# State-space tables of a four-layer trunk: angles doubled inclusively, powers alike, and the early table work reordered

## The reference, cut to what matters

```
step    = exp(log_step)[:, None]                  # 64 groups of 16 channels
lam_bar = exp((a_re + i a_im) * step)             # 64 groups x 64 states, complex
b_bar   = ((lam_bar - 1) / lam)[..., None] * b
bu      = einsum('gpc,sbgc->sbgp', b_bar, u)
states  = associative_scan(x_t = lam_bar * x_{t-1} + bu_t)      # over 256 tokens
y       = real(einsum('gcp,sbgp->sbgc', c, states)) + d_skip * h
z       = gelu(y) @ w_glu + b_glu;  out = z1 * sigmoid(z2)
```

## Time and profile before

| | us |
|---|---|
| median of 3 runs | 1458.84 (1455.54 to 1459.17) |
| the profiled execution's own time | 1456.15 |
| its span | 1454.4 |
| PE busy | 1388.9 (95%) |
| DVE busy | 1015.8 (70%) |
| ACT busy | 801.8 (55%) |
| POOL busy | 654.3 (45%) |

### The profile page before, as it was taken

The page is one execution under the profiler, slowest core; times in us unless marked ns, Lnnn a source line. Parts: engine busy times, 40 slices in busy tenths (PEclk is TensorE's granted clock), DMA queues, the critical chain, the costliest instruction groups (busy, mean ns, idle before and its releaser), DMA issues.

```text
span 1454.4 us, 33002 instructions
## 1 busy us (share of the span) xinstructions
PE 1388.9 (95%) x13677; PEld 1308.2 (90%) x13677; DVE 1015.8 (70%) x1613; ACT 801.8 (55%) x1336; POOL 654.3 (45%) x391
## 2 busy tenths in 40 slices
PE   8999999999998988999998679999999999999998
PEld 8999999989787777999987669999989998999988
DVE  6774987735595465897778776887755675788841
ACT  5586665635551334665653445665655468575642
POOL 4343365541006102495568753365554232355553
PEclk9999999999999999999999799999999999999999
DMA  6533465553433001485554005465555553455553
GB/s 202 187 126 107 155 204 173 182 195 116 144 128 106 5 4 60 145 234 174 182 173 137 2 3 164 156 203 174 178 192 160 160 159 100 152 185 173 187 172 106
DMA packets 208168, 209.59 MB, mean 144 GB/s; under 512 B 7954, under 2 KB 207170, under 8 KB 208034
## 3 DMA queue, kind: packets, MB, share of 16 engines
q1 hardware_dynamic: 207168, 206.21, 43.9%
q0 software_dynamic: 800, 1.46, 0.5%
q10 hardware_dynamic: 66, 0.02, 0.0%
HBM read 206.62 MB, written 1.05 MB: 143 GB/s over the span
## 4 chain that ended last, share of the span: by engine, by line
PE 81%; DVE 9%; ACT 4%; POOL 3%; issue 2%; DMA 0%; ACTq 0%; DVEq 0%; POOLq 0%
PE psum L422 17%; PE psum L424 17%; PE psum L423 17%; PE psum L818 7%; PE psum L599 5%; PE psum L820 4%; DVE x_low L551 2%; POOL work L2422 1%; ACT w_high L397 1%; PE psum L1751 1%; PE psum L1765 1%; DVE work L536 1%; DVE w_low L405 1%; PE psum L1083 1%; PE psum L2568 1%
## 5 line engine op out<-in xcount | busy, mean ns | idle before, releaser
L405 POOL TENSOR_TENSOR w_low<-ring,w_high 128x1024 fp32r<-128x1024 f32 (+1 forms) x185 | 459.1, 2483 | 662.3 <-ACT w_high L397 662.1
L397 ACT ACTIVATE w_high<-ring 128x1024 fp32r<-128x1024 f32 (+1 forms) x368 | 376.4, 1037 | 216.7 <-PE psum L424 124.5
L422 PE MATMUL psum<-x_high,w_high 128*128 128x256 f32 x1728 | 491.0, 284 | 3.6 <-DVE w_low L405 1.4
L424 PE MATMUL psum<-x_high,w_low 128*128 128x256 f32 x1728 | 488.9, 283 | 0.0
L423 PE MATMUL psum<-x_low,w_high 128*128 128x256 f32 x1728 | 488.9, 283 | 0.0
L405 DVE TENSOR_TENSOR w_low<-ring,w_high 128x1024 fp32r<-128x1024 f32 x183 | 296.2, 1620 | 172.9 <-ACT w_high L397 171.7
L422 PEld LDWEIGHTS psum<-x_high,w_high 128*128 128x128 f32 x1728 | 331.6, 192 | 6.0 <-issue 3.1
L423 PEld LDWEIGHTS psum<-x_low,w_high 128*128 128x128 f32 x1728 | 331.7, 192 | 0.0
L424 PEld LDWEIGHTS psum<-x_high,w_low 128*128 128x128 f32 x1728 | 331.6, 192 | 0.0
L818 PE MATMUL psum<-inner,w_high 128*128 128x512 f32 x528 | 187.0, 399 | 0.9 <-DVE w_low L405 0.9
L931 DVE SCALAR_TENSOR_TENSOR work<-psum,par,work 128x255 f32<-128x255 f32 (+1 forms) x352 | 144.6, 472 | 45.9 <-ACT work L850 45.7
(11 more groups left out here) (351 smaller groups left out, 2223.5 us busy)
## 6 DMA issues: line engine op xcount, KB each, us to landing
ring<-in_ffn_w_up_dram SPq DMA_DIRECT2D x88, 1024.0 KB, 5.1
ring<-in_ffn_w_down_dram SPq DMA_DIRECT2D x32, 1024.0 KB, 5.0
ring<-in_dsa_w_in_dram SPq DMA_DIRECT2D x28, 1024.0 KB, 5.2
ring<-in_ffn_w_down_dram SPq DMA_DIRECT2D x16, 768.0 KB, 4.3
ring<-in_rwkv_w_rkv_dram SPq DMA_DIRECT2D x12, 1024.0 KB, 5.0
ring<-in_dsa_w_out_dram SPq DMA_DIRECT2D x8, 1024.0 KB, 5.0
ring<-in_s_w_glu_dram SPq DMA_DIRECT2D x8, 1024.0 KB, 5.3
ring<-in_rwkv_w_out_dram SPq DMA_DIRECT2D x4, 1024.0 KB, 4.9
```

The source lines that it names most:

```text
L397: act.activation(high, raw, ACT.Copy).then_inc(sem("w_rounded", b), 1)
L405: eng.tensor_tensor(low, raw, high.bitcast(F32), ALU.subtract).then_inc(sem("w_split", b), 1)
L422: pe.matmul(out_, lhs[0], rhs[0], start=start, stop=False, skip_group_check=True)
L424: return pe.matmul(out_, lhs[1], rhs[0], start=False, stop=stop, skip_group_check=True)
```

## The change

The grid and the powers are both held as one table with real and imaginary part side by side, and doubled "inclusively": the last entry that is already there is the factor for the next ones, so that no squared factor is kept. A doubling is two multiplications over both parts at once and two sums. The grid's doublings go into parts 5 to 9 (1 and 2 in part 5, 4 in part 6, 8 in part 7; the last one's products in part 8 and its sums in part 9), and its temporary moves to slot 9, so ACT's copies into that slot now wait for `fill_added` 1. `products(1)` moves out of part 10 to a place behind the MLP and ahead of the norm's reciprocal; `coefs(1)` moves behind the norm's scaling. The scan's first turn waits for `fill_added` 1 instead of 3. The four idle transposes go from this norm and stay in layer 1's.

```diff
@@ norm_mean
                 if c == 1:
-                    idle_turns(pe, 4, 3)
+                    idle_turns(pe, 4 if trailing else 0, 3)
@@
-        grid_tmp = work[:, 14, 1536:2048]
+        grid_tmp = work[:, 9, 0:1024]
-        LAST_PART = 11
+        LAST_PART = 10
@@ first_angle
-            for x, value in zip(grid, (1.0, 0.0)):
-                pool_step.mark(pool.memset(x[:, :, 0:1], value))
             pool.wait_ge(sem("angles_ready"), 3)
-            for x, u in ((L8_RE, U_RE), (L8_IM, U_IM)):
-                pool_step.mark(pool.tensor_copy(small(x), small(u + S5_L - 1)))
+            for v, value in ((0, 1.0), (1, 0.0)):
+                pool_step.mark(pool.memset(grid[:, v, :, 0:1], value))
+                pool_step.mark(pool.tensor_copy(grid[:, v, :, 1:2], small((U_RE, U_IM)[v] + S5_L - 1).unsqueeze(2)))
...
+        def angle_products(pool, have):
+            n = min(have, S5_N - 1 - have)
+            shape = [P, 2, S5_H, n]
+            x, dst = grid[:, :, :, 1:1 + n], grid[:, :, :, have + 1:have + 1 + n]
+            t = grid_tmp[:, 0:2 * S5_H * n].rearrange("p (v g n) -> p v g n", v=2, n=n)
+            for out_, v in ((dst, 0), (t, 1)):
+                factor = grid[:, v, :, have:have + 1].unsqueeze(1).to_broadcast(shape)
+                pool_step.mark(pool.tensor_tensor(out_, x, factor, ALU.mult))
             pool.wait_ge(pool_step.sem, pool_step.n)
...
+        def angle_sums(pool, have):
...
+            for v, op in ((0, ALU.subtract), (1, ALU.add)):
+                pool_step.mark(pool.tensor_tensor(dst[:, v], dst[:, v], t[:, 1 - v], op))
+            pool.wait_ge(pool_step.sem, pool_step.n)
@@ s5_angles
-            if part == 6:
+            if part == 5:
                 first_angle(pool)
-                for half in range(2):
-                    double(pool, 1, half)
-            for p, have in ((7, 2), (8, 4), (9, 8)):
+            for p, have in ((5, 1), (5, 2), (6, 4), (7, 8)):
                 if part == p:
-                    square_angle(pool)
-                    for half in range(2):
-                        double(pool, have, half)
+                    angle_products(pool, have)
+                    angle_sums(pool, have)
+            if part == 8:
+                angle_products(pool, S5_N // 2)
             if part == 9:
-                square_angle(pool)
+                angle_sums(pool, S5_N // 2)
@@ s5_pool
-                if f == 1:
-                    for half in range(2):
-                        double(pool, S5_N // 2, half)
@@ s5_act
                 copy_turned_table(i)
+            act.wait_ge(sem("fill_added"), 1)
@@ s5_math: complex_product (six operations) becomes
+            def next_powers(have, last):
...
+                for out_, v in ((dst, 0), (t, 1)):
+                    factor = both[:, v, have - 1:have].unsqueeze(1).to_broadcast([P, 2, have, S5_H])
+                    step.mark(dve.tensor_tensor(out_, x, factor, ALU.mult))
+                dve.wait_ge(step.sem, step.n)
+                tt(dst[:, 0], dst[:, 0], t[:, 1], ALU.subtract)
+                ins = dve.tensor_tensor(dst[:, 1], dst[:, 1], t[:, 0], ALU.add)
@@ s5_tables
-            if part == 10:
-                products(dve, 1)
-                coefs(dve, 1)
@@ turned_in
-                    dve.wait_ge(sem("fill_added"), 3)
+                    dve.wait_ge(sem("fill_added"), 1)
@@ s5_dve
+            coefs(dve, 1)
             products(dve, 2)
@@ the vector engine's program
                 if L % 3 == 2:
+                    products(dve, 1)
                     norm_scale(dve, norm_index(L, 0), "norm_mix", L, in_psum=IN_PSUM)
```

More of the change, by code:

```diff
@@ L2293, in trunk @@
         V_all = work[:, 9, :].rearrange("p (q r z) -> p q r z", q=4, r=2)
-        grid = [work[:, 13, i * 1024:(i + 1) * 1024].rearrange("p (g n) -> p g n", n=S5_N) for i in (0, 1)]
+        grid = work[:, 13, :].rearrange("p (v g n) -> p v g n", v=2, n=S5_N)
         cos_n, sin_n = (work[:, 13, i * 1024:(i + 1) * 1024].rearrange("p (q z) -> p q z", q=4) for i in (0, 1))
         coef = work[:, 14, 0:1536].rearrange("p (v k g) -> p v k g", v=6, k=S5_L)
-        grid_tmp = work[:, 14, 1536:2048]
+        grid_tmp = work[:, 9, 0:1024]
         with_cos = work[:, 8, 0:512].rearrange("p (r z) -> p r z", r=2)
@@ L2313, in trunk @@
         A_RE, A_IM, STEP, SIGMA, TH, TURNS, ANGLE, CO_ARG, DEN, B_RE, B_IM, TMP = range(12)
-        U_RE, U_IM, GROW, MAG_N, MAG_P, L8_RE, L8_IM, ANGLE_A, ANGLE_B = 12, 20, 28, 36, 44, 52, 53, 54, 55
+        U_RE, U_IM, GROW, MAG_N, MAG_P = 12, 20, 28, 36, 44
         FB_RE, FB_DIFF, FB_SUM, GC_RE, GC_DIFF, GC_SUM = range(6)
         S5_DMAS = (6, 4, 4)
-        LAST_PART = 11
+        LAST_PART = 10
         FT_BANKS = (4, 5)
@@ L2373, in first_angle @@
             pool.wait_ge(pool_step.sem, pool_step.n)
[L2375 to L2382, removed]
-            pool.wait_ge(pool_step.sem, pool_step.n)
-            pool.wait_ge(pool_step.sem,
-                         pool_step.mark(pool.tensor_tensor(dst, dst, t, (ALU.subtract, ALU.add)[half])))
@@ L2396, in s5_angles @@
+        def angle_sums(pool, have):
+            n = min(have, S5_N - 1 - have)
+            dst = grid[:, :, :, have + 1:have + 1 + n]
+            t = grid_tmp[:, 0:2 * S5_H * n].rearrange("p (v g n) -> p v g n", v=2, n=n)
+            for v, op in ((0, ALU.subtract), (1, ALU.add)):
+                pool_step.mark(pool.tensor_tensor(dst[:, v], dst[:, v], t[:, 1 - v], op))
+            pool.wait_ge(pool_step.sem, pool_step.n)
         def s5_angles(pool, part):
@@ L2681, in ts @@
                 then(dve.tensor_scalar(out_, x, a, b, op0, op1))
[L2683 to L2690, removed]
+            def next_powers(have, last):
+                both = work[:, 6, U_RE * S5_H:(U_IM + S5_L) * S5_H].rearrange("p (v k g) -> p v k g", v=2, k=S5_L)
+                x, dst = both[:, :, 0:have], both[:, :, have:2 * have]
+                t = table(GROW, 2 * have).rearrange("p (v k) g -> p v k g", v=2)
+                for out_, v in ((dst, 0), (t, 1)):
[4 more added lines that the diff above has]
+                ins = dve.tensor_tensor(dst[:, 1], dst[:, 1], t[:, 0], ALU.add)
                 if last:
@@ L2695, in complex_product @@
                     then(ins)
-            return then, tt, ts, complex_product
+            return then, tt, ts, next_powers
         def s5_tables(dve, part):
-            then, tt, ts, complex_product = s5_math(dve)
+            then, tt, ts, next_powers = s5_math(dve)
             if part == 0:
@@ L2727, in s5_tables @@
                 if part == p:
-                    last = [table(x + have - 1, 1).to_broadcast([P, have, S5_H]) for x in (U_RE, U_IM)]
-                    complex_product(table(U_RE + have, have), table(U_IM + have, have),
-                                    (table(U_RE, have), table(U_IM, have)), last, table(GROW, have), have == 4)
+                    next_powers(have, have == 4)
             if part == 5:
```

## The result

| | median, us | runs | ratio to before (95% interval) |
|---|---|---|---|
| before | 1458.06 | 20 | |
| changed | 1462.5 | 20 | 1.0025 (1.0016 to 1.0034) |

The forecast was 1451 (1446 to 1456), 6.5 us faster. It came out 3.6 us slower by the ratio (0.0025 x 1458; its interval is 2.3 to 5.0 us), and the medians lie 4.4 us apart. This is at the 4.4 us that I had called a measurement's limit, but twenty runs on each side leave no doubt that it is slower.

The account below looks back on a forecast made before the run. PE bounds the whole span, but POOL's table chain bounds the S5 layer's start. States(0) 8.9 us earlier, less 1.0 for the clock and 1.4 for the port, gives 6.5 us off the 1457.4 mean: 1451 (1446 to 1456).

Parts of the forecast that it names:

- POOL's chain: S5 layer's start: less table work before fill 0 and between fills 0 and 1, 12.1 us off the way to fill 1.
- `products(1)` ahead of the reciprocal: In the norm: moved `products(1)` ends at 795.4, the reciprocal waits 1.5 us for it, scaling ends 4.8 us earlier.
- The second, the port: Second cost, beside POOL's parts 5 to 8: DVE's tables end 0 to 4 us later; 1.4 us taken.
- The adding of squares starts at 789.2 and ends at 790.9: DVE ahead of the norm: with `products(1)` gone from part 10, the squares are added from 789.2 to 790.9.
- PE's split waits: PE's waits for weight splits: the 0.4 us for POOL's goes; of DVE's, 0 to 0.9 us comes back, 0 taken.
- The powers: DVE's tables: six dependent operations become two products and two sums, three times; gain 0 to 0.9 us, 0 taken.
- The tie at 754.3: DVE, with its powers some 2 us shorter, is ready at about 754.3, at the same time as POOL's split.
- The clock: PE in the S5 start: turns of hT at half clock cost 2.8 us, states(0) may regain 1.5; cost taken 1.0.
- port lock: Rival: DVE ends its tables 4 us later, PE starves for splits, norm starts 4 us later; 1452.5 to 1455.3, chance 0.15.
- the four signs of being wrong: 960-column POOL products well above 2 us; more than three split waits; reciprocal after 798; half clock in turns of hT.

Follow-up runs that it names:

- g_squares: The changed kernel with one more wait: POOL's additions of fill 0 wait until VectorE has added the squares; ratio to before 0.9994.
- p_powers_old: The changed kernel with the powers doubled as before, in six dependent operations instead of four; ratio to before 1.0040.
- f_best: The changed kernel with last doubling between fills 1 and 2, fill 0 held until squares are added, VectorE's temporary and B coefficients in PSUM; ratio to before 0.9957.
- k_warm: f_best with 40 idle turns on PE in its three waits in the S5 start; ratio to before 0.9931.
- s_early: f_best without POOL's wait for the squares; VectorE adds the squares ahead of products(0) instead; ratio to before 0.9944.
- w_both: s_early with the idle turns of k_warm; ratio to before 0.9913.

## Why the prediction was wrong, step by step

1. **POOL's chain (12.1 us off the way to fill 1): right in what it takes away.** Nobody waits for fill 1 in the changed kernel. An undisturbed product of 960 columns took 1.92 us against my 1.80. Beside DVE the prices did not hold: parts 7 and 8 took 5.3 and 5.0 us on POOL, for 3.7 and 3.6. Fill 0's additions started at 797.5 on the old scale and not at 789, since they wait for DVE's `products(0)`.
2. **`products(1)` ahead of the reciprocal: right.** The reciprocal waited 0.22 us for the root and starts where `products(1)` ends. I had 14.6 us from the residual's end to states(0) (791.9 to 806.5). It measured 14.9.
3. **"The second, the port ... I take 1.4": this step failed.** I said that DVE's tables could end up to 4 us later, 2.5 of it in part 8 and 1.5 before. They ended 9.3 us later (796.50 less 4.25, against 782.92 before): part 8 began 5.1 later (787.27 less 4.25, against 777.93) and took 4.2 more (9.19 against 4.95). The mechanism was the one named, and its place too. The size was off. Before part 8, DVE's weight splits read two SBUF tiles as well and three of them took 3.3 to 3.5 us instead of 1.2, and part 7's four operations took 4.53 us, for 1.84 before. In part 8 I charged a split and two products of 1.8. What stood there were products of 2.5, the split and also part 9's two sums (2.54). POOL's queue had no gap between 765.6 and 795.7, and from 776 on nearly every operation of DVE with two SBUF inputs paid for one of POOL's.
4. **"The adding of squares starts at 789.2 and ends at 790.9": this step failed.** The same sum let fill 0 start "from about 789" on POOL, beside it, and I did not put the two rows together. Both read two SBUF tiles. The squares took 4.79 us, 3.1 more. `g_squares` shows that this alone was worth 2.5 us of stage.
5. **PE's split waits: wrong.** I let the 0.4 us for POOL go, which it did, and left DVE's at 1.8. They grew to 9.4. The longest, 5.41 us, is for the split at 797.82, which took 0.95 us itself but stood behind part 8. The sum had no term for it, and none for the half clock behind it.
6. **The powers (I took 0, with 0.9 as the other end): too low, but inside what I gave.** `p_powers_old` puts the powers themselves at 0.8 us, and the whole of its stage at 2.2. The tie at 754.3 was lost to POOL, as the row of 3.48 us for the split behind the powers shows, the first of VectorE's timeline above, and the gain came all the same.
7. **The clock (1.0 of net cost): not where I looked.** The turns of hT ran in 3.73 us, as before, and states(0) in 2.23, near the 2.06 of full clock. The half clock came ahead of them, at the end of the down projection and in the norm's eight matmuls (3.68 us, for 1.99 in `f_best`), where `products(1)` on DVE hid all but 0.22 us of it. It came again right behind them, in the lag tables (3.45 us, for 2.06 at full clock) and states(1) (3.63). `k_warm` puts what idle turns win back in `f_best` at about 2.5 us of stage.

The sums close. I had the residual's last sum at 791.9. It ended at 803.9 on the old scale, 12.0 us later: 9.3 and 3.1 of points 3 and 4, less some 0.4, nearly all of it the wait for PE's last matmul that I had left to DVE. Behind it I was off by 0.3. So the port cost 12 us on the path where I took 1.4, and turned a forecast gain into a loss.

The rival "port lock" had the mechanism and the sign of the step, but ended at 2 to 5 us of gain, since it was built from the same too small size. What the prediction lacked was the sum over all of DVE's operations with two SBUF inputs between 765 and 805, each against the length of the POOL operation beside it. Of the four signs of being wrong that it names, three came: products of 960 columns at 2.50 us, a fourth wait for a split, and a reciprocal at 807.5 on the old scale. The fourth, half clock in the turns of hT, did not.

That the powers are worth anything, and the gains of `k_warm` and `s_early` over `f_best`, stay near the limit of what these runs can tell. That `w_both` gains on `k_warm` (0.9931 to 0.9913) is likewise inside their intervals.

## What to carry to other kernels

When work is moved or merged on POOL, list what VectorE runs beside it with two SBUF inputs, the squares and splits of other stages included, and charge each such operation the length of the POOL operation next to it, and the matrix engine the clock that it loses in the wait that follows. Fewer and longer POOL operations can cost more than many short ones, though POOL itself is done sooner. Place long POOL work where VectorE reads PSUM or is idle, or put one operand of VectorE's operations in PSUM; then look whether the held-back work has become the next wait.

## What the runs showed of the hardware

- A VectorE operation of 256 columns with two SBUF inputs took 2.0 to 2.1 us beside back-to-back POOL operations, 0.43 alone, and 0.42 beside them when one input was in PSUM.
- The lock works both ways: POOL's product of 960 columns took 2.50 us with such VectorE operations around it and 1.92 without.
- Eight POOL products of 240 columns took 6.75 us, two of 960 took 5.00 in the same place. The eight let VectorE's six operations through in 4.7 us, the two in 9.2.
- With 40 idle transposes in three waits, sixteen of them in the 2.1 us wait right ahead of states(0), the granted clock was 1.00 there and its 64 matmuls ran in 2.06 us. Without them it was 0.50 and they took 3.63.
- After a wait of 5.41 us PE ran 24 matmuls of 256 columns in 5.27 us (granted clock 0.50), then 0.12 us apart again.
